# Last layer: the output gate's projection of blocks one to five in seven products of halves instead of eight

## The reference, cut to what matters

```
def odd_layer(z, w_in, conv_w, conv_b, w_a, b_a, w_x, b_x, lam, w_out):
    zp = jnp.einsum('btd,de->bte', z, w_in)          # 1024 -> 2048 + 2048
    u, gate = split_cols(zp, ODD_SPLITS)
    ...                                              # xc: four-tap convolution of u
    y = (lru_direction(xc, ..., reverse=False) + lru_direction(xc, ..., reverse=True))
    y = y * jax.nn.silu(gate)
    return jnp.einsum('bte,ed->btd', y, w_out)
```

## Time and profile before

| what | value |
|---|---|
| median of 3 runs | 1793.42 us |
| the profiled execution: its own time | 1796.17 us |
| its span | 1794.4 us |
| PE busy | 1772.7 us (99% of the span) |
| DVE busy | 774.5 us (43%) |
| ACT busy | 444.2 us (25%) |
| POOL busy | 109.0 us (6%) |
| DMA q1, share of 16 engines | 69.3% |
| granted clock of PE | 1.0 of full speed |

### The profile page before, as it was taken

The page is one execution under the profiler, slowest core; times in us unless marked ns, Lnnn a source line. Parts: engine busy times, 40 slices in busy tenths (PEclk is TensorE's granted clock), DMA queues, the critical chain, the costliest instruction groups (busy, mean ns, idle before and its releaser), DMA issues.

```text
span 1794.4 us, 21955 instructions
## 1 busy us (share of the span) xinstructions
PE 1772.7 (99%) x8876; PEld 1008.6 (56%) x8911; DVE 774.5 (43%) x1761; ACT 444.2 (25%) x954; POOL 109.0 (6%) x94
## 2 busy tenths in 40 slices
PE   9999999999999999999999999999999999999999
PEld 8999754444344334775444434433366767468874
DVE  3678753222221213856322222121345566334775
ACT  2333211111111101143111111110135534217770
POOL 2212000000000000000000000000011100001110
DMA  9623669999999999348999999999931332041520
GB/s 387 264 102 132 249 280 403 422 427 427 427 427 428 428 427 426 163 165 354 396 428 426 428 428 426 428 428 427 422 144 75 143 139 94 18 174 44 240 89 23
DMA packets 41831, 527.45 MB, mean 294 GB/s; under 512 B 4800, under 2 KB 5472, under 8 KB 8576
## 3 DMA queue, kind: packets, MB, share of 16 engines
q1 hardware_dynamic: 39200, 516.70, 69.3%
q10 hardware_dynamic: 2528, 9.31, 1.3%
HBM read 524.91 MB, written 1.08 MB: 293 GB/s over the span
## 4 chain that ended last, share of the span: by engine, by line
PE 84%; DMA 12%; DVE 2%; SPq 1%; issue 0%; ACT 0%; POOL 0%; DVEq 0%; ACTq 0%
PE ps L213 26%; PE ps L943 19%; PE ps L978 10%; DMA ring<-in_wu 8%; PE ps L877 4%; PE ps L995 3%; PE ps L1165 3%; PE ps L782 2%; DMA ring<-in_w_lat 2%; PE ps L671 2%; PE ps L1806 2%; DMA ring<-in_w_qkv 2%; PE ps L1774 2%; PE ps L1338 1%; PE ps L746 1%; PE ps L1821 1%
## 5 line engine op out<-in xcount | busy, mean ns | idle before, releaser
L943 PE MATMUL ps<-ring,work 128*64 128x512 f32 x1856 | 409.3, 593 | 6.0 <-DMA ring<-in_wu 5.9
L943 PEld LDWEIGHTS ps<-ring,work 128*64 128x64 f32 x1856 | 131.4, 137 | 271.1 <-issue 249.9
L213 PE MATMUL ps<-xl,ring 128*128 128x256 f32 (+3 forms) x1152 | 249.1, 374 | 0.0
L213 PEld LDWEIGHTS ps<-xl,ring 128*128 128x128 f32 x1152 | 207.7, 190 | 34.5 <-issue 2.5
L978 PE MATMUL ps<-ring,work 128*64 128x512 f32 x816 | 181.5, 594 | 0.1
L2771 DVE TENSOR_TENSOR work<-work,ps 128x512 f32<-128x512 f32 x32 | 22.0, 688 | 362.4 <-PE ps L943 342.7
L3382 POOL TENSOR_TENSOR small<-small,halves 128x1 f32<-128x1 f32 (+4 forms) x42 | 45.8, 1089 | 1430.3 <-DVE small L2573 937.8
L978 PEld LDWEIGHTS ps<-ring,work 128*64 128x64 f32 x816 | 56.2, 137 | 100.3 <-issue 99.0
L213 PE MATMUL ps<-ring,xl 128*128 128x256 f32 (+1 forms) x416 | 106.1, 412 | 0.0
L2732 DVE SCALAR_TENSOR_TENSOR work<-ps,small,big 128x512 f32<-128x512 f32 x60 | 45.0, 750 | 135.9 <-ACT big L2028 135.9
L2013 ACT COPY work<-ps 128x512 f32<-128x512 f32 x32 | 18.8, 586 | 307.5 <-PE ps L950 307.5
(11 more groups left out here) (528 smaller groups left out, 2245.8 us busy)
## 6 DMA issues: line engine op xcount, KB each, us to landing
ring<-in_wg SPq DMA_DIRECT2D x62, 2048.0 KB, 21.4
ring<-in_wu SPq DMA_DIRECT2D x52, 2048.0 KB, 22.2
ring<-in_wd SPq DMA_DIRECT2D x48, 2048.0 KB, 23.6
xl<-in_wd SPq DMA_DIRECT2D x10, 2048.0 KB, 24.0
xl<-in_wu SPq DMA_DIRECT2D x9, 2048.0 KB, 19.4
ring<-in_w_odd SPq DMA_DIRECT2D x8, 2048.0 KB, 7.7
ring<-in_w_xz SPq DMA_DIRECT2D x7, 2048.0 KB, 19.7
ring<-in_w_qkv SPq DMA_DIRECT2D x6, 2048.0 KB, 35.4
```

Source lines behind the costliest of these rows:

```text
L213: i = e.matmul(bout, lhs(k), rhs(k), start=start and k == ks[0], stop=stop and k == ks[-1])
L943: last = e.matmul(b[64 * j:64 * j + 64, :], x[:, 4 * a + k, 64 * j:64 * j + 64], w[k // 2][:, 2 * (k % 2) + j, :], start=a + k == 0, stop= ...
```

## The change

For blocks 1 to 5 the output gate's 1024 x 256 weights and 1024 x 256 inputs are taken as halves: two halves of the model dimension, two of the channels, two of the tokens. The eight products of halves become seven, with sums of weights and inputs in four of them. The input sums t1 to t4 are made once, on DVE (`vector_odd_sums`), the weights' sums g1 to g4 for each of the five blocks, on POOL, in `lnb`. DVE puts the products together (`vector_odd_halved`, in five instructions) into `sgt`, and ACT applies the silu there, in place and one block later (`scalar_odd_halved`). Now the `og` banks of these blocks are freed by DVE. The sums t1a and t1 of the output projection's weights move from the beginning of DVE's turn `cb` 5 to its end.

```diff
+        HALVED = range(1, 6)
+        oc_in = Sig(gained.sem, [(0, 0), (0, 1), ("x",)] + [k for cb in range(1, 8) for k in [(cb, 0), (cb, 1)] + (
+            [("og", cb, 0), ("og", cb, 1)] if cb in HALVED else [])], gained)
...
+        gsums = [area(lnb[:, :, :].rearrange("p a n -> p (a n)"), 512 * i, (4, 128)) for i in range(4)]
+        hsums = [area(big, 8 * 272 + 512 * i, (4, 128)) for i in range(4)]
...
+        def tensor_odd_halved(e, cb):
+            s1, s2, s3, s4 = gsums
+            t1, t2, t3, t4 = hsums
+            for j, products in enumerate((((gw2(cb, 0, 0), xo2(0, 0)), (gw2(cb, 0, 1), xo2(1, 0)), (s2, t2)),
+                                          ((s1, t1), (s3, t3), (s4, xo2(1, 1)), (gw2(cb, 1, 1), t4)))):
+                b, gone = eb.take(("og", cb, j), oc_in("og", cb, j))
+                if gone:
+                    e.wait_ge(*gone)
+                for i, (w, x) in enumerate(products):
+                    if (j, i) == (0, 2):
+                        e.wait_ge(*oc_in("x"))
+                        e.wait_ge(*ix_in("s", cb))
+                    for k in range(4):
+                        last = e.matmul(b[:, 128 * i:128 * i + 128], w[:, k, :], x[:, k, :], start=k == 0, stop=k == 3)
+                last.then_inc(*og_mm.up(cb, j))
...
-                    tensor_odd_gate(e, cb + 1)
+                    if cb + 1 in HALVED:
+                        tensor_odd_halved(e, cb + 1)
+                    else:
+                        tensor_odd_gate(e, cb + 1)
...
+        def scalar_odd_halved(e, cb):
+            e.wait_ge(*oc_in("og", cb, 1))
+            for j in range(2):
+                o = sgt[cb % 2][:, j, 16:272]
+                e.activation(o, o, ACT.Silu).then_inc(*og_in.up(cb, j))
...
                 if cb:
                     scalar_root(e, cb - 1)
-                if cb < 7:
+                if cb in HALVED:
+                    scalar_odd_halved(e, cb)
+                if cb < 7 and cb + 1 not in HALVED:
                     scalar_odd_gate(e, cb + 1)
...
+        def vector_odd_sums(e):
+            t1, t2, t3, t4 = hsums
+            e.wait_ge(*zT_in(1, 1, 1))
+            e.tensor_tensor(t1, xo2(0, 1), xo2(0, 0), ALU.subtract).then_inc(*vs.up())
...
+            e.tensor_tensor(t4, xo2(1, 0), t2, ALU.subtract).then_inc(*oc_in.up("x"))
+
+        def vector_odd_halved(e, cb):
+            o, a, b = sgt[cb % 2], eb["og", cb, 0], eb["og", cb, 1]
...
+            e.wait_ge(*og_mm(cb, 0))
+            if cb > 1:
+                e.wait_ge(*y_in(cb - 2))
+            e.tensor_copy(o[:, 1, 144:272], a[:, 0:128]).then_inc(*vs.up())
+            e.wait_ge(*vs())
+            e.tensor_tensor(first, two(a[:, 128:384]), bc(o[:, 1, 144:272], 1, 2), ALU.add).then_inc(*oc_in.up("og", cb, 0))
+            e.wait_ge(*og_mm(cb, 1))
+            e.wait_ge(*oc_in("og", cb, 0))
+            e.tensor_tensor(second, two(b[:, 0:256]), bc(o[:, 1, 16:144], 1, 2), ALU.add).then_inc(*vs.up())
+            e.wait_ge(*vs())
+            e.tensor_tensor(across, two(b[:, 256:512]), second, ALU.add).then_inc(*vs.up())
+            e.wait_ge(*vs())
+            e.tensor_tensor(o[:, 1, 144:272], o[:, 1, 144:272], b[:, 0:128], ALU.add).then_inc(*oc_in.up("og", cb, 1))
...
             vector_odd_conv(e, 0)
+            vector_odd_sums(e)
...
                 if cb:
                     vector_odd_scan(e, cb - 1)
+                if cb + 1 in HALVED:
+                    vector_odd_halved(e, cb + 1)
                 vector_odd_square(e, cb)
+                if cb == 5:
...                                                  # t1a and t1, moved here
...
+            g1, g2, g3, g4 = gsums
             for cb in range(8):
+                if cb + 1 in HALVED:
+                    e.wait_ge(*ring("ow", cb + 1))
+                    if cb:
+                        e.wait_ge(*og_mm(cb, 1))
+                    e.tensor_tensor(g1, gw2(cb + 1, 1, 0), gw2(cb + 1, 1, 1), ALU.add).then_inc(*gs.up())
+                    e.tensor_tensor(g3, gw2(cb + 1, 0, 0), gw2(cb + 1, 1, 0), ALU.subtract).then_inc(*gs.up())
+                    e.wait_ge(*gs())
+                    e.tensor_tensor(g2, g1, gw2(cb + 1, 0, 0), ALU.subtract).then_inc(*gs.up())
+                    e.wait_ge(*gs())
+                    e.tensor_tensor(g4, gw2(cb + 1, 0, 1), g2, ALU.subtract).then_inc(*ix_in.up("s", cb + 1))
```

More of the change, by code:

```diff
@@ L341, in build @@
         odd_mix = then(mix, ("t1a", "t1", "t3", "s1", "s3", "r11", "s2", "t2", "r22", "s4", "t4", "r12", "r21", "r2b"))
-        oc_in, sq_in, b_in, y_in = then(gained, G8, range(2)), then(xd_in, G8), then(dec_d, G8), then(dec_in, G8)
+        HALVED = range(1, 6)
+        oc_in = Sig(gained.sem, [(0, 0), (0, 1), ("x",)] + [k for cb in range(1, 8) for k in [(cb, 0), (cb, 1)] + (
+            [("og", cb, 0), ("og", cb, 1)] if cb in HALVED else [])], gained)
+        sq_in, b_in, y_in = then(xd_in, G8), then(dec_d, G8), then(dec_in, G8)
         oo_in = Sig(yv_in.sem, [x[0:3] for x in OUT], yv_in)
         og_in, lr_in, lt_in = then(zs_in, G8, range(2)), then(mx_in, G8, G8), then(Bl_in, G8)
-        la_in, rt_in, ix_in = then(dec_e, G8), then(S0_in, G8), then(y_rs, G8)
+        la_in, rt_in = then(dec_e, G8), then(S0_in, G8)
+        ix_in = Sig(y_rs.sem, [k for cb in G8 for k in ([("s", cb + 1)] if cb + 1 in HALVED else []) + [(cb,)]], y_rs)
         class Ring:
@@ L584, in build, with gw2, xo2 @@
         wsum2 = [lnb[:, :, :].rearrange("p a n -> p (a n)"), area(work, 6528, (1024,))]
+        gsums = [area(lnb[:, :, :].rearrange("p a n -> p (a n)"), 512 * i, (4, 128)) for i in range(4)]
+        hsums = [area(big, 8 * 272 + 512 * i, (4, 128)) for i in range(4)]
+        def gw2(cb, j, half):
+            return kview(8, 512)(ring.view("ow", cb))[:, 4 * half:4 * half + 4, 256 + 128 * j:384 + 128 * j]
+        def xo2(half, t):
+            return xT[:, 4 * half:4 * half + 4, 16 + 128 * t:144 + 128 * t]
         def oo(hf, n):
@@ L3259, in vector_odd_conv @@
                     a.then_inc(*(oc_in.up(cb, j) if tap == 3 else vs.up()))
+        def vector_odd_sums(e):
+            t1, t2, t3, t4 = hsums
+            e.wait_ge(*zT_in(1, 1, 1))
+            e.tensor_tensor(t1, xo2(0, 1), xo2(0, 0), ALU.subtract).then_inc(*vs.up())
+            e.tensor_tensor(t3, xo2(1, 1), xo2(0, 1), ALU.subtract).then_inc(*vs.up())
+            e.wait_ge(*vs())
+            e.tensor_tensor(t2, xo2(1, 1), t1, ALU.subtract).then_inc(*vs.up())
+            e.wait_ge(*vs())
+            e.tensor_tensor(t4, xo2(1, 0), t2, ALU.subtract).then_inc(*oc_in.up("x"))
+        def vector_odd_halved(e, cb):
+            o, a, b = sgt[cb % 2], eb["og", cb, 0], eb["og", cb, 1]
+            two = lambda x: x.rearrange("p (i n) -> p i n", i=2)
+            first, second = o[:, :, 16:144], o[:, :, 144:272]
+            across = two(o[:, :, :].rearrange("p j n -> p (j n)")[:, 144:432])[:, :, 0:128]
+            e.wait_ge(*og_mm(cb, 0))
[7 more added lines that the diff above has]
+            e.tensor_tensor(second, two(b[:, 0:256]), bc(o[:, 1, 16:144], 1, 2), ALU.add).then_inc(*vs.up())
+            e.wait_ge(*vs())
+            e.tensor_tensor(across, two(b[:, 256:512]), second, ALU.add).then_inc(*vs.up())
+            e.wait_ge(*vs())
+            e.tensor_tensor(o[:, 1, 144:272], o[:, 1, 144:272], b[:, 0:128], ALU.add).then_inc(*oc_in.up("og", cb, 1))
         def vector_odd_square(e, cb):
@@ L3329, in vector_odd @@
             vector_odd_conv(e, 0)
+            vector_odd_sums(e)
             for cb in range(8):
[L3331 to L3337, removed]
+                if cb == 6:
                     e.wait_ge(*ring("oo", 1, 1))
@@ L3346, in vector_odd @@
                     vector_odd_scan(e, cb - 1)
+                if cb + 1 in HALVED:
+                    vector_odd_halved(e, cb + 1)
                 vector_odd_square(e, cb)
+                if cb == 5:
+                    e.wait_ge(*ring("oo", 0, 0))
+                    e.wait_ge(*ring("oo", 0, 1))
+                    e.tensor_tensor(wsum2[0], oflat(0, 1, 0, 2048), oflat(0, 0, 0, 2048), ALU.subtract
+                                    ).then_inc(*odd_mix.up("t1a"))
+                    e.tensor_tensor(wsum2[1], oflat(0, 1, 2048), oflat(0, 0, 2048), ALU.subtract).then_inc(*odd_mix.up("t1"))
             vector_odd_mixed(e)
```

## The result

The changed kernel takes 1798.57 us (median of 11 runs, 1797.84 to 1800.49), the kernel before 1793.81 beside it (11 runs, 1793.07 to 1794.34). The ratio is 1.0028, 95% interval 1.0020 to 1.0036: slower by 4.8 us, where +1.6 was forecast, and just above the range's end of 1798.3. The profiled execution took 1799.02 us, its span is 1797.2, and PE's granted clock is 1.0 of full speed in the mean.

A forecast was written before the change was run, and what follows sets the result against it. PE was taken to bound the kernel, busy in 1772.7 of 1794.4 us. The terms -3.3 saved, +4.1 at the gates, +0.5 at the beginning and +0.3 at p1 gave +1.6, or 1795.0 us; range 1790.9 to 1798.3.

The forecast's parts named there:

- the end of the chain for `t3`: At p1 after block 7's gates: PE waits for `y_in(5)`, late through `t3`; 0.3 us lost, G6 being block 6's gates' start.
- Hidden: Other engines' work in the loop: ACT's later silu, POOL's sums and DVE's square cost PE nothing.
- The gates' term: Gates of blocks 2 to 5: PE waits for DVE, held by POOL's sums at 2 to 4; 4.1 us lost, bounds 0 and 7.8.
- The beginning: Layer's start: POOL's g1 for block 1 holds DVE's L3021, so PE's L1358 starts late; 0.5 us lost, or nothing.
- the bound by L2506: Layer's start: L3021 is held until g1 ends, as L2506 was held elsewhere; 0.5 us, the other bound being nothing.
- The saving: PE's projection of blocks 1 to 5: 6.25 us for 6.91, so 0.66 a block, 3.3 for five.
- A: Rival at the gates: DVE isn't held by POOL; -1.8 us, 1791.6, or 1790.1 if nothing is lost; chance 0.25.
- B: Rival at the gates: POOL's two sums run back to back ahead of L3293; +5.3 us, 1798.7; chance 0.15.
- C: Rival in the projection: products of halves are slower for more strided operands; saving nil at 0.123 a record, 1798.3; chance 0.05.
- The chance of slower: Whole kernel measured over 1797.0 us, through B, part of C and the forecast's tail; chance 0.15.

The follow-up runs named there:

- e2: Changed kernel with `t3` moved from ahead of block 7's convolution to behind s3 in `vector_odd_mix`: 1795.83 us, ratio 1.0013 to the kernel before.
- e3: Changed kernel with a third `sgt` buffer, so silus wait for `y_in(cb - 3)`, `t3` left in place: 1796.16 us, ratio 1.0013 to the kernel before.
- e5: Changed kernel with `t1a` and `t1` back at the beginning of DVE's turn 5: 1798.01 us, ratio 1.0022 to the kernel before.
- e8: Changed kernel with only block 1 in seven products of halves: 1797.0 us, ratio 1.0018 to the kernel before.
- e1: Changed kernel with POOL's sums for blocks 3, 4 and 5 waiting for the scan's last product: 1796.31 us, ratio 1.0014 to the kernel before.
- e4: Changed kernel with POOL's first sums, for block 1, waiting until the whole input is in `xT`: 1798.37 us, ratio 1.0026 to the kernel before.
- e6: Changed kernel with three `sgt`, `t3` behind s3, block 1's sums later, DVE's five instructions between the scans and their sum: 1793.61 us, ratio 0.9998 to before.
- e9: e6's kernel with POOL's sums for blocks 2 to 5 also waiting for DVE's square of the block before: 1790.76 us, ratio 0.9982 to the kernel before.

## Why the prediction was wrong

**The step that failed** is the end of the chain for `t3`: "PE's p1 needs it at 17.8 + 3.56 = G6 + 21.4: 0.3 lost with the restart. Bounds: 0 if POOL is behind `t3` (then 19.4), 0.8." Everything up to it held: POOL's L3546 stood before `t3`, `t3` got 2.1 us longer (2.2 forecast), and `y_in(5)` was there at 1741.93, 21.41 behind G6 (21.5 forecast). But p1 is not the reader that counts. Another is ACT's silu of block 7, which overwrites the `sgt` buffer that L3363 of block 5 reads and waits for it (`y_in(cb - 2)` in `scalar_odd_gate`, a wait that my description of the kernel leaves out). Two things hang on the silu. It frees the two `og` banks for the gates' products 6 and 7. And on ACT itself the table load and the sigmoids of block 7 come behind it, the first of which frees p1's bank: that is the later of the two, since p1 starts 0.04 behind that sigmoid's end. Under "Hidden" I looked at ACT's silu for the halved blocks only, and those of blocks 6 and 7 are not halved. The earlier trace rows shows that ACT has no slack of its own there: L2300 starts 0.04 behind the end of L3293, idle for 2.61 until just that ("[2.61 <-DVE big L3293]"); block 7's does the same in the trace of before:

```profile
1738.89 0.66 ACT L2300 ACTIVATE work<-ps 128x256 f32<-128x256 f32 x2 [2.61 <-DVE big L3293]
...
1740.86 1.60 ACT L2314 ACTIVATE work<-ps,col 128x272 f32<-128x272 f32 x4
```

The term would have come out so. In the trace of before `y_in(5)` is there at 0.65 behind block 7's gates; my own 21.5 behind G6 is 3.7 behind them, so 3.05 later. The first sigmoid of block 7, of some 0.5, ends at about 1741.36, and p1 starts at 1741.77: 0.4 of slack. 3.05 - 0.4 = 2.65, where 2.6 was measured. I gave it 0.3, and the bounds of 0 and 0.8 were drawn for the wrong reader. e2 takes the whole loss away, e3 2.2 of it with `y_in(5)` as late as ever, and e5 and e8 show the same chain elsewhere. The 0.4 that e3 leaves is what p1's own wait is worth, near the 0.3 of the forecast. That one term is 2.3 of the 3.2 us between forecast and clock.

**The gates' term** had the right mechanism and a size too small: 4.8 for 4.1, within its bounds. The port's part was right to a hundredth (L3363 1.64 for 0.69; e1 takes it away). The rest, 0.49 without POOL, was put at 0.31. At block 5's gates the copy starts 0.10 behind L3363's end, where I had 0.03, L3322 to L3325 is 0.53 for 0.45, and the other gaps are 0.01 or 0.02 longer: L3329 ends at G + 3.47 for G + 3.29. L3320 and L3325 wait for two semaphores each, the others for one; e3 shows that 0.2 goes when L3320's wait for the scan's last has ended long before, and for L3325 the reason is not shown.

**The beginning** was 0.4 for 0.5 (e4), and the held instruction has one SBUF input, as the bound by L2506 had it. The saving was 0.65 to 0.66 a block (6.25 for 6.91, turns of 17.15 for 17.80).

**The rivals.** A (DVE not held) and B (POOL's two sums back to back) both fall by L3363: 1.64 us, not 0.69, and not 2.9; the second sum started at 1648.12, behind L3363. C (slower products) falls by 6.25. By its time B's 1798.7 is the nearest, and it is wrong all the same. The chance of slower, 0.15, was too low because every case was a sum over PE's direct waits for DVE; none had a term for what goes through ACT.

**The rule on the port.** What the changed kernel, e1, e4, e6 and e9 show is: of a DVE instruction with two inputs in SBUF and a POOL sum the later one gets longer by nearly the whole overlap, whichever it is (L3363 by 0.95 for 1.09 of overlap, POOL's L3539 by 0.44 for 0.59), and so does a tensor_scalar with one input in SBUF (L3061, 1.75 for 0.75). DVE's sums with one input in PSUM don't (0.42 beside POOL's). The Trainium skill (SBUF — State Buffer, "Who interferes with whom") states that a DVE instruction with two SBUF inputs contends with a GpSimd instruction that reads SBUF, and that copies and tensor_scalar can contend too, in a mode that uses both ports. These runs agree with it, but for the 0.14 or 0.15 by which the cost stays below the overlap.

## What to carry to other kernels

When something makes a signal later, list every wait on it, on all engines, and for each what it frees in turn; the reader that you think of first may have slack while another, with a two-deep buffer, has none; here an idle time of ACT that ended 0.04 behind its releaser was the mark of it. Put GpSimd's work beside VectorE instructions that read PSUM, not beside those that read SBUF: here the same sums cost 3 us in one place and nothing in the other. And after moving an engine's work, add up its whole turn with the stretched durations; in e6 the gain at the gates of block 2 was given back at those of blocks 3 and 4, because DVE's own turn had become longer than PE's.

## What the runs showed of the hardware that I had not expected

The holding goes both ways and adds up. In e6 DVE's and POOL's instructions took turns one by one: POOL's product of 1088 columns took 3.54 us for 2.49, and DVE's SCALAR_TENSOR_TENSOR of as many 3.46 for 1.29. A scan (TENSOR_TENSOR_SCAN, 256 columns) is held as well, 1.69 for 0.67. And when one engine has been waiting, it comes ahead of the other's next instruction, even one that depends on nothing: POOL's second sum stood behind L3363 and took 1.71 for 1.27.

PE's clock can fall behind such a wait, which the account above leaves out. In the profiled execution of e4 (1800.17, the longest of its nine) PE had the full clock up to its waits for ACT before p1 (1.26 and 0.92); right behind them the granted clock was at the lower of its two levels (0.50 of full from 1745 to 1747, 0.65 and 0.64 as means of the microsecond before and behind), and from p1 to the end of the span it took 54.4 for the 52.7 of the changed kernel's trace. In the four kernels that wait there (the changed one, e1, e4, e8) 14 of 42 executions have a mean granted clock of 0.999 and not 1.0, nearly all of them the longest of their kernel; in the seven other experiments it is 5 of 76. That the clock fell at this wait in all 14 is not shown.
